# Three token blocks' activations from dense products, or two and the third from fetched rows

## The reference, cut to what matters

```
q = (x_blk @ w_q).reshape(n, PEER_HEADS, 2, PEER_HALF)
s = einsum('nhpc,hpkc->nhpk', q, keys)                  # 8 heads, 2 halves, 128 keys
top_s, top_i = top_k(s, 16)
cand_s = top_s[:, :, 0, :, None] + top_s[:, :, 1, None, :]    # 16 x 16 sums
best_s, best_c = top_k(cand_s, 16)                            # 16 experts a head
gate = softmax(best_s)
act = gelu(einsum('nhkd,nd->nhk', expert_u[idx], x_blk))
out = einsum('nhk,nhkd->nd', gate * act, expert_v[idx])
```

## Time and profile before

| | |
|---|---|
| median of 3 runs | 1715.44 us (1713.63 to 1715.93) |
| span of the profiled execution | 1714.0 us, 24432 instructions |
| TensorE (PE) busy | 1690.2 us, 99% |
| VectorE (DVE) busy | 1327.7 us, 77% |
| ScalarE (ACT), GpSimd (POOL) busy | 782.1 us and 785.5 us, 46% each |
| moved | 413.88 MB, mean 241 GB/s |

### The profile page before, as it was taken

One profiled execution on the slowest core, in us unless ns is written; L12 is line 12 of the kernel. 1 busy time (PEld: TensorE's weight loads), 2 busy tenths in 40 slices (PEclk: granted clock), 3 DMA queues, 4 the chain that ended last, 5 costly groups with the idle time before them and its releaser, 6 DMA issues.

```text
span 1714.0 us, 24432 instructions
## 1 busy us (share of the span) xinstructions
PE 1690.2 (99%) x9073; PEld 1510.9 (88%) x9073; DVE 1327.7 (77%) x1864; ACT 782.1 (46%) x1132; POOL 785.5 (46%) x494
## 2 busy tenths in 40 slices
PE   8999999999999999999999999999999999999998
PEld 6887788878899999999999999999888888888886
DVE  3666622265898999989999889976888888888887
ACT  6444433344333666746666566654323323323223
POOL 4333243333702555655555777771463443433430
PEclk9999999999999999999999999999999999999999
DMA  5222233322336666686667988888999999999992
GB/s 160 75 73 86 62 87 98 91 85 82 111 112 219 219 221 228 232 312 205 227 234 243 357 287 295 295 307 306 394 387 396 393 382 383 389 374 390 383 388 89
DMA packets 212443, 413.88 MB, mean 241 GB/s; under 512 B 11520, under 2 KB 150816, under 8 KB 207008
## 3 DMA queue, kind: packets, MB, share of 16 engines
q1 hardware_dynamic: 156880, 253.51, 42.4%
q0 software_dynamic: 36864, 134.23, 21.7%
q10 hardware_dynamic: 18640, 25.45, 4.2%
HBM read 360.73 MB, written 52.43 MB: 241 GB/s over the span
## 4 chain that ended last, share of the span: by engine, by line
PE 91%; DVE 5%; ACT 2%; issue 1%; DMA 0%; ACTq 0%; SPq 0%; DVEq 0%
PE psum L1375 30%; PE psum L1316 29%; PE psum L284 20%; PE psum L1306 6%; PE psum L1343 2%; PE psum L358 1%; PE psum L512 1%; DVE ul L1571 1%; DVE hot L1634 1%; PE psum L372 1%; PE psum L345 1%; DVE ring L1646 1%; DVE hot L1636 0%; DMA acc<-in_x 0%; ACT xTh L546 0%
## 5 line engine op out<-in xcount | busy, mean ns | idle before, releaser
L1316 PE MATMUL psum<-xnTh,uh 128*128 128x384 f32 x1024 | 353.8, 345 | 3.3 <-DVE ul L1571 3.1
L1316 PE MATMUL psum<-xnTl,uh 128*128 128x384 f32 x1024 | 343.4, 335 | 0.0
L1316 PE MATMUL psum<-xnTh,ul 128*128 128x384 f32 x1024 | 343.4, 335 | 0.0
L236 POOL TENSOR_TENSOR wl<-raw,wh 128x1024 fp32r<-128x1024 f32 x72 | 176.4, 2455 | 280.0 <-ACT wh L586 279.5
L1375 PE MATMUL psum<-vh,dwh 128*128 128x512 f32 x768 | 298.8, 389 | 0.2 <-DVE dwl L1664 0.2
L1375 PE MATMUL psum<-vh,dwl 128*128 128x512 f32 x768 | 298.8, 389 | 0.0
L1375 PE MATMUL psum<-vl,dwh 128*128 128x512 f32 x768 | 298.8, 389 | 0.0
L1530 POOL DMA_INDIRECT ring<-in_expert_v,index x128 | 170.9, 1335 | 248.9 <-DVE acc L1651 207.5
L1448 ACT ACTIVATE vh<-v_raw 128x4096 fp32r<-128x4096 f32 x31 | 112.7, 3635 | 339.0 <-PE psum L1375 338.5
L1530 POOL DMA_INDIRECT ring<-in_expert_u,index x128 | 176.1, 1375 | 165.0 <-DVE ring L1646 92.3
L1646 DVE SCALAR_TENSOR_TENSOR ring<-ring,x 128x1024 f32<-128x1024 f32 x128 | 209.7, 1659 | 6.4 <-DMA ring<-in_expert_u,index 5.1
(11 more groups left out here) (230 smaller groups left out, 2925.0 us busy)
## 6 DMA issues: line engine op xcount, KB each, us to landing
u_raw<-in_expert_u SPq DMA_DIRECT2D x128, 512.0 KB, 3.9
v_raw<-in_expert_v SPq DMA_DIRECT2D x30, 2048.0 KB, 14.6
expert_act<-hb ACTq DMA_DIRECT2D x128, 192.0 KB
expert_gate<-grid SPq DMA_DIRECT2D x12, 2048.0 KB, 7.2
dh<-expert_act SPq DMA_DIRECT2D x32, 768.0 KB, 5.6
dg<-expert_gate SPq DMA_DIRECT2D x32, 768.0 KB
raw<-in_w_in SPq DMA_DIRECT2D x40, 512.0 KB, 3.8
raw<-in_w_q SPq DMA_DIRECT2D x16, 512.0 KB, 3.9
```

Of the source, the lines that this page charges most:

```text
L236: nc.gpsimd.tensor_tensor(wl[slot][:], raw[slot][:], wh[slot][:].bitcast(F), ALU.subtract).then_inc(w_lo[slot], 1)
L1316: last = nc.tensor.matmul(zb[s][:, 0:DT], w[s][:, c, :], x[:, c, 0:DT], start=(c == 0 and i == 0), stop=(c == C - 1 and i == 2))
```

## The change

The third block (`MIXED`) takes its activations from fetched rows of `expert_u`, like the fourth; its weighted sum stays in the dense downward stage. So the upward stage has `UT` = 256 tokens in place of 384. VectorE handles 256 rows as dots and 128 as sums (before 128 and 128). The third block's gates are multiplied with its 128 activations before they are spread (`gate_rows`), and the downward stage takes its grid as weights as it stands.

The low part of the rows comes from TensorE and ScalarE: `take_high` adds minus the high part, which is a matmul with a negated identity (`minus`), onto the transposed rows in PSUM, in the middle of the step's products, and ScalarE's new `low` copies the rest. The gate spread is one fp32 matmul of 128 columns a token, without high and low parts; VectorE makes both 0/1 rows, ScalarE multiplies one by the gate in fp32 (`weigh_hots`), and `evac` copies straight into the grid, of which there are two. GpSimd has only the fetches left.

The first block's turn is at step 36 with a batch every second step; the second and third have theirs at 76 and 100 with a batch every step. The second stage of the ranking looks at 112 cells in place of 256 (all 16 columns for the first 4 rows, 4 columns for the other 12), and `cells` finds row and column of a cell.

```diff
-FIRST, EVERY = 12, 36
 EACH_BLOCK = P // 8
 BATCHES = DT // 8
+TURN = (36, 76, 100)
+EVERY = (2, 1, 1)
...
-    return FIRST + EVERY * (k // EACH_BLOCK) + 2 * (k % EACH_BLOCK) + 2
+    b = k // EACH_BLOCK
+    return TURN[b] + 2 + EVERY[b] * (k % EACH_BLOCK)
+
+
+def spread_step(x):
+
+    return hot_step(x // 2) + 2 + (x % 2 if EVERY[x // (2 * EACH_BLOCK)] == 2 else 0)
...
-    if n in HOT or n in GATED_OUT and GATED_OUT[n] != SPARSE or n > 123:
-        return 1
...
+    if n < 63:
+        return 1 if n % 6 == 0 else 2
+    if n < 72:
         return 0
...
+    return 3 if n % 4 == 0 else 2
...
+        def take_high(n, q=0):
+
             s = n % 2
...
+            pe.wait_ge(ut_hi[s], q * 2 + (n // 2 + 1))
+            for half in range(2):
+                last = nc.tensor.matmul(utp[s][:, half * T:(half + 1) * T], minus[:], uh[s][:, 4 * half:4 * half + 4, :],
+                                        start=False, stop=True, skip_group_check=True)
+            last.then_inc(ut_sub[s], 1)
...
             transposes(n + 1, q)
-            products(n, q)
+            products(n, q, range(0, C // 2))
+            take_high(n + 1, q)
+            products(n, q, range(C // 2, C))
...
+        def spreads(b, q):
+            n0, k0 = TURN[b] + 4, EACH_BLOCK * b
             for n in range(4):
-                step(n, q)
+                step(n0 + n, q)
+                if EVERY[b] == 2:
+                    spread(k0 + n // 2, n % 2, q)
+                else:
+                    for half in range(2):
+                        spread(k0 + n, half, 2 * q)
...
+        def low(n):
+            s, r = n % 2, n // 2
+
+            act.wait_ge(ut_sub[s], r + 1)
+            if n == 0:
+                act.wait_ge(w_made[1], tiles + PRIMED)
+            nc.scalar.activation(ul[s][:].rearrange("p c f -> p (c f)"), utp[s], ACT.Copy).then_inc(ut_lo[s], 1)
...
+        def weigh_hots(k):
             s = k % 2
 
             act.wait_ge(S["hot_eq"], k + 1)
             for n in range(8):
                 t = 8 * k + n
-                last = nc.scalar.activation(hot[s][:, n, 1, :], hot[s][:, n, 2, :].bitcast(F), ACT.Copy,
-                                            scale=gate_hi[:, t:t + 1].bitcast(F))
-            last.then_inc(hot_hi[s], 1)
+                last = nc.scalar.activation(hot[s][:, n, 1, :], hot[s][:, n, 1, :], ACT.Copy, scale=selT[:, 2, t:t + 1])
+            last.then_inc(hot_ready[s], 1)
...
             if n + 1 < STEPS:
                 high(n + 1)
+                low(n + 1)
             if n in HOT:
-                hi(HOT[n])
+                weigh_hots(HOT[n])
             gelu(n)
...
             dve.wait_ge(g_full[s], k // 2 * 2 + PRIMED)
-            nc.vector.tensor_tensor(hot[s][:, :, 2, :], selT[:, 1, cols].unsqueeze(2).broadcast_to([P, 8, KEYS]), keys_,
-                                    ALU.is_equal).then_inc(S["hot_eq"], 1)
```

More of the change, by code:

```diff
@@ L84, in mix_program @@
 def mix_program(nc, sem, psum, m, a, acc, sT, xnT, const, u_raw, u_in, u_view, ut_full, score, rank, gain, st):
[L87 to L88 removed]
+    ident, iota, tri, ones, causal, gap, vecs, minus = (const[k] for k in (
+        "ident", "iota", "tri", "ones", "causal", "gap", "vecs", "minus"))
     xh, xl = sT
@@ L523, in mix_tensor @@
             query(i)
-        pe.wait_ge(S["row"], ROW1 + DB)
-        for b in range(DB):
+        pe.wait_ge(S["row"], ROW1 + UB)
+        for b in range(UB):
             last = nc.tensor.transpose(av[:, b * P:(b + 1) * P], rb[:, b, :], ident[:])
@@ L1165, in experts_program @@
-    ul = [m.put(f"ul{i}", kb, [P, C, P], R) for i, kb in enumerate((112, 132))]
-    hb = [m.put(f"hb{i}", 144 + 1.5 * i, [P, DT]) for i in range(2)]
-    grid = m.put("grid", 16, [P, KEYS, 32])
-    parts = [m.put(f"parts{i}", 116 + 4 * i, [P, 4, 2, KEYS]) for i in range(2)]
-    hot = [m.put(f"hot{i}", kb, [P, 8, 3, KEYS], R) for i, kb in enumerate((152, 32))]
-    sel = m.put("sel", 80, [P, 2, 3, HEADS * TOPK])
-    total = m.put("total", 83, [P, 2, HEADS])
+    uh = [m.put(f"uh{i}", kb, [P, C, P], R) for i, kb in enumerate((116, 128))]
@@ L1172, in experts_program @@
+    ul = [m.put(f"ul{i}", kb, [P, C, P], R) for i, kb in enumerate((120, 132))]
+    hb = [m.put(f"hb{i}", 144 + i, [P, UT]) for i in range(2)]
+    grid = [m.put(f"grid{i}", kb, [P, KEYS, 32]) for i, kb in enumerate((16, 92))]
+    hot = [m.put(f"hot{i}", kb, [P, 8, 2, KEYS]) for i, kb in enumerate((152, 32))]
+    sel = m.put("sel", 68, [P, NB, 3, HEADS * TOPK])
+    total = m.put("total", 185.5, [P, 2, HEADS])
     eq = m.put("eq", 76, [P, HEADS * TOPK // 2, TOPK])
-    selT = m.put("selT", 180, [P, 2, DT])
@@ L1297, in experts_sync, with first_low @@
         sp_.wait_ge(Z["out"], (NB + 1) * 16)
+    def first_low():
+        nc.tensor.wait_ge(ut_hi[0], 1)
+        for half in range(2):
+            last = nc.tensor.matmul(utp[0][:, half * T:(half + 1) * T], minus[:], uh[0][:, 4 * half:4 * half + 4, :],
+                                    start=False, stop=True, skip_group_check=True)
+        last.then_inc(ut_sub[0], 1)
     def experts_tensor(pe):
@@ L1315, in products @@
+        def products(n, q=0, chunks=range(C)):
+            s = n % 2
+            if 0 in chunks:
+                pe.wait_ge(ut_lo[s], q * 2 + (n // 2 + 1))
+                pe.wait_ge(h_done[s], q * 2 + (n // 2 + PRIMED))
+            for c in chunks:
                 for i, (w, x) in enumerate(((uh, xh), (uh, xl), (ul, xh))):
-                    last = nc.tensor.matmul(zb[s][:, 0:DT], w[s][:, c, :], x[:, c, 0:DT],
+                    last = nc.tensor.matmul(zb[s][:, 0:UT], w[s][:, c, :], x[:, c, 0:UT],
@@ L1345, in spread, with steps @@
             last.then_inc(g_full[s], 1)
-        with pe.Fori(0, FIRST // 4) as q:
+        def spreads(b, q):
+            n0, k0 = TURN[b] + 4, EACH_BLOCK * b
             for n in range(4):
-                step(n, q)
+                step(n0 + n, q)
+                if EVERY[b] == 2:
+                    spread(k0 + n // 2, n % 2, q)
+                else:
+                    for half in range(2):
+                        spread(k0 + n, half, 2 * q)
+        def steps(first, last):
+            with pe.Fori(0, (last - first) // 4) as q:
+                for n in range(4):
+                    step(first + n, q)
@@ L1355, in experts_tensor @@
                 step(n)
-            with pe.Fori(0, 8) as q:
-                for n in range(4):
-                    step(n0 + 4 + n, q)
-                    spread(32 * b + n, q)
-        for n in range(FIRST + EVERY * DB, STEPS - 1):
+            quads = EACH_BLOCK * EVERY[b] // 4
+            with pe.Fori(0, quads) as q:
+                spreads(b, q)
+            at = n0 + 4 + 4 * quads
+            if b < DB - 1 and at < TURN[b + 1]:
+                steps(at, TURN[b + 1])
+        for n in range(at, STEPS - 1):
             step(n)
```

486 lines of the change are left out of this document (247 added, 239 removed).

## The result

The changed kernel takes **1937.05 us** (median of 4 runs, 1935.31 to 1940.26), the kernel before 1715.32 beside it: a ratio of 1.1296 with a 95% interval of 1.128 to 1.1312. The forecast was 1869 with a range of 1815 to 1930. So the sign and the mechanism came as written, and the time lies 68 us above the forecast, outside the range.

What follows compares the result with a forecast made beforehand. TensorE was taken to bound the kernel before. Span 1714.0, plus 111 for the upward stage, 0.6 for the first low part and 42 for the clock, gave 1867.6; the median 1.4 above made 1869 us, range 1815 to 1930.

Steps and rivals of the forecast that it cites:

- The loop: Second and third blocks' upward steps: TensorE, VectorE and ScalarE wait in series, 11.4 us a step, TensorE's work 5.85.
- Rivals 3: Upward stage: VectorE's pair need not wait for the same step's spread, TensorE's columns decide; 1646 us, chance 0.08.
- the three waits: Second and third blocks: L1345 waits for high, ScalarE's hot rows for VectorE's pair, that pair for TensorE's spread.
- rival 4: Second and third blocks: VectorE off the path, ScalarE's chain alone left, 6.9 us a step; 1701 us, chance 0.04.
- The clock: TensorE's granted clock falls after idling in second and third blocks' loops, costing 1.5 us each, 28 x 1.5 = +42.
- Plain step: Upward steps without hot rows or spreads: TensorE's own 4.15 us decides, with no wait; 58 of them.
- first block: Upward stage, a batch every second step: two steps take 11.4 us, where two cost 11.06 before.
- exponentials: Upward stage: table loads with one exponential take 3.0 us, some 2.7 stays on slackless ScalarE, three times 8.
- a 512-wide copy 0.49: ScalarE's grid copy in the spread steps: 0.49 us each, two in the loop taken as 0.98.
- I put 0: Downward stage: stays under TensorE, no change; 0 to 15 us if the DMA engines' thin cover goes.
- Rival 2: Upward stage: low clock on all the path, +48, and in the first block, +22; 1939 us, chance 0.09.
- VectorE's one-hots: Upward stage: a one-hot half takes 1.22 us, without GpSimd's work beside which it took up to 2.32.

Runs made afterwards that it cites:

- e1: Changed kernel with the second and third blocks' spreads one step behind the hot rows instead of two, same work; 1765.34 us.
- e8: Changed kernel with e1's order of spreads and e2's contiguous grid copies together; 1739.71 us.
- e3: Changed kernel with 36 unread 256-column matmuls before `take_high` in the second and third blocks' steps; 1933.91 us.
- e6: Changed kernel with 51 unread 256-column matmuls before `take_high` in the second and third blocks' steps; 1918.33 us.
- e2: Changed kernel with grid copies writing 512 contiguous elements instead of every 32nd, grid in another order; 1926.06 us.
- e10: e4 with 211 row dots in the upward stage instead of 203, more of them in early steps, ended in step 119; 1669.46 us.
- e4: Changed kernel with one 128x1024 VectorE product behind its pair replacing ScalarE's eight hot rows; 1690.29 us.

## Why the prediction was right and wrong

**The loop: right.** Rivals 3 and 4 are excluded by the three waits and by e1, where the same work in another order gives rival 4's loop (7.76 with the strided copies, and in e8 6.86 for its 6.9). The parts of the 13.72 us (timeline above) beside those of the prediction: pair and products 3.37 for 1.86, spreads 1.99 for 1.90, VectorE's pair 2.39 for 2.36, hot rows 2.35 for 2.47, Gelu 0.83 for 0.86, two copies **1.69 for 0.98**, high 1.10 for 1.08. Six of seven stand to 0.15, once the first is taken with the clock's 1.5.

**The clock: right, its size in part by luck.** The granted clock had a mean of 0.75 in these loops, half of the time at 1.2 GHz, more than half of that while TensorE stood idle, with products 0.213 apart until 1014.24 and 0.12 after it, and cost 1.51 in pair and products of the loop, against 1.5 put. e3's loops with and without the fall differ by 1.55, e6 puts 1.25 on it. But where the low stretch lies against the work was nothing that the prediction could know: in e2, with copies as cheap as it had them, the same two terms took 6.05 (3.58 + 2.47) for its 3.76, 2.29 more. By the Trainium skill, TensorE: Matmul & The Clock Gate, section What's actually happening, the low level is the default and activity releases it; by that rule, the trace agrees, as fillers without meaning brought it back.

**Plain step and first block: 4.19 for 4.15, pairs of steps 11.93 for 11.4.** The latter is 6.73 + 5.20; the long one holds a strided copy as well.

**Where the 71 us of span come from** (1938.5 against 1867.6; the median of the runs lies 1.4 below its span, where I had it 1.4 above). The start of the stage gives 0.5. The upward stage gives 51, of which I count, from the starts of the L1345 pairs:

- 28 loops 384.5 instead of 28 x 12.9 = 361.2: +23. By the parts above it is the two strided copies, 28 x 0.71 = 20. But e2, without the stride, has 377.9, still 16.7 over, since the low clock then lay on more of the work: of these 23, the copies and the clock can't be told apart;
- the steps at both ends of the two blocks, 50.6 for 47.0: +4;
- first block 15 x 0.53: +8, plain steps 58 x 0.04: +2;
- exponentials: the pairs of steps 7.25 + 5.87, 6.96 + 5.89 and 7.89 + 5.84 in place of three times 8.38 are 14.6 for 8.1: +6;
- Gelu waiting for the transfer of `expert_act` in three steps: +6. I had given ScalarE's queue no transfer that could be late, though the kernel before has one such wait, of 3.3 us;
- the first preparation of the downward stage (L1523, 1.9 us on ScalarE in two steps), which ScalarE's slack had hidden before: +3.

That makes 52, 1 more than the stage's 51. The downward stage gives 14.7 and the end 5.1.

**The step that failed** in size is thus first "a 512-wide copy 0.49": the row was that of a contiguous output, and the copy in the loop writes every 32nd element. It takes 0.84 (1.69 for two). e8 shows its whole price coming back where the clock is full (25.6 us against e1), e2 only 11 of 25 where it is not. The prediction put it in a rival, as 28 x 1.0, not in the sum: its place on the path was certain from the order, and only its size was not. Second, "I put 0" for the downward stage with "0 to 15 us if it goes": it went in full. The cause of 8 of the 14.7 us stands in the trace, a fetched row that came late; that the rest is of the same kind, e10 beside e4 makes likely. I had counted the bytes per round and not the moment at which the dots need them, and taken 211 dots in the upward stage from the limit `IN_UP`, where the steps' own counts add to 203, so that eight more were left for the downward stage; and the end behind the last matmul, which waits on VectorE's sums, had no term. Third, what lies on ScalarE beside the loop (exponentials, `expert_act`, L1523), 15 us, when the text itself said that ScalarE has no slack.

**Rival 2** named 1939, within 2 us of the result, but not by its reasons: its 22 for the first block at a lower clock did not come, since the clock is 1.00 from 668 to 850. Its +48 and the stride were there, as 35 to 42 and 20; the rest is the list above. That it comes so close is luck.

**VectorE's one-hots: right.** The pair kept 1.22 in each of its 48 batches; the view of the instructions of L1701 has

```profile
L1701 DVE TENSOR_TENSOR hot<-selT,iota x48: 1219/1226/1226, 652.9 to 1330.7; 128x1024 f32<-128x1024 f32 x48
```

with no trace of the 2.32 of the earlier trace rows. GpSimd has only transfers to issue in this stage. By the Trainium skill, SBUF — State Buffer, section SBUF: two separate sides, VectorE with two SBUF inputs and a GpSimd operation that reads SBUF shut each other out; by that rule, the trace agrees.
